# Where the weight sums of the seven-product stages are made: from SBUF during the second block to a table in HBM during the first

## The reference

```
for l in range(2):                       # first block
    h = rmsnorm(x); proj = h @ w_in[l]   # q k v g, sb sc sx, ca cb, three gates of 1024
    y_ret, y_sc, y_cf = retention(q,k,v), short conv, long conv + layernorm
    merged = sum of sigmoid(gate_b) * (y_b @ w_b)
    x = x + rmsnorm(merged @ w_o[l])
    up = causal_dwconv(rmsnorm(x) @ w_up[l])
    x = x + rmsnorm((silu(gate) * val) @ w_down[l])
for l in range(2):                       # second block
    h = rmsnorm(x); proj = h @ w_in_2[l] # u v z_a, c_q c_kv k_rope z_b, x_c z_c, g_a g_b g_c
    y_a = gmlp_spatial(u, v) * silu(z_a)
    y_b = mla_attention(c_q, c_kv, k_rope) * silu(z_b)
    y_c = rg_lru(x_c) * silu(z_c)
    merged = sum of sigmoid(g_b) * (y_b @ w_proj_b)
    x = x + rmsnorm(merged @ w_out[l])
```

## Time and profile before

| | us |
|---|---|
| median of 3 runs | 3138.83 |
| lowest and highest | 3138.8, 3139.8 |
| the profiled execution, its own time | 3137.91 |
| its span in the trace | 3136.6 |
| PE busy | 3120.1 |
| PEld, DVE, ACT, POOL busy | 2636.8, 1981.9, 1328.2, 574.4 |

### The profile page before, as it was taken

One profiled execution on the slowest core, in us unless ns is written; L12 is line 12 of the kernel. 1 busy time (PEld: TensorE's weight loads), 2 busy tenths in 40 slices (PEclk: granted clock), 3 DMA queues, 4 the chain that ended last, 5 costly groups with the idle time before them and its releaser, 6 DMA issues.

```text
span 3136.6 us, 38506 instructions
## 1 busy us (share of the span) xinstructions
PE 3120.1 (99%) x15368; PEld 2636.8 (84%) x15368; DVE 1981.9 (63%) x2664; ACT 1328.2 (42%) x2075; POOL 574.4 (18%) x427
## 2 busy tenths in 40 slices
PE   9999999999999999999999999999999999999999
PEld 8888888888888888888888888888888878888887
DVE  6876456665687655656558765457856766455774
ACT  4333334344333334433445542236745544233762
POOL 1201212110020111111013330130221332131031
PEclk9999999999999999999999999999999999999999
DMA  4322223235442233232552263223442254223423
GB/s 169 118 97 98 96 100 108 94 111 204 150 121 94 94 101 113 89 101 94 201 172 89 92 179 101 85 98 114 124 172 96 86 150 133 95 87 101 139 96 135
DMA packets 109938, 368.39 MB, mean 117 GB/s; under 512 B 14336, under 2 KB 14592, under 8 KB 108480
## 3 DMA queue, kind: packets, MB, share of 16 engines
q1 hardware_dynamic: 101280, 326.37, 31.5%
q0 software_dynamic: 8336, 39.03, 4.2%
q10 hardware_dynamic: 144, 0.52, 0.1%
HBM read 343.32 MB, written 6.29 MB: 111 GB/s over the span
## 4 chain that ended last, share of the span: by engine, by line
PE 95%; DVE 2%; DMA 1%; ACT 1%; issue 1%; POOL 0%; SPq 0%; ACTq 0%; POOLq 0%
PE ps L651 94%; DMA f<-wst 1%; PE ps L742 1%; PE ps L1067 0%; DVE r L1821 0%; DVE wl L1811 0%; ACT wh L1194 0%; DVE f L1826 0%; DMA X<-x_in 0%; DVE f L1889 0%; ACT f L1607 0%; SPq L2784 0%; DVE sm L2329 0%; POOL f L2718 0%; DVE r L2303 0%
## 5 line engine op out<-in xcount | busy, mean ns | idle before, releaser
L651 PE MATMUL ps<-h,wh 128*128 128x512 f32 (+1 forms) x5696 | 1609.5, 368 | 0.7
L651 PEld LDWEIGHTS ps<-h,wh 128*128 128x128 f32 x5696 | 1029.9, 188 | 182.2 <-issue 3.4
L651 PE MATMUL ps<-h,wl 128*128 128x512 f32 (+1 forms) x2848 | 1046.1, 367 | 0.0
L1811 DVE TENSOR_TENSOR wl<-raw,wh 128x1024 fp32r<-128x1024 f32 (+2 forms) x547 | 683.0, 1259 | 229.8 <-ACT wh L1194 229.2
L1194 ACT CAST wh<-raw 128x1024 fp32r<-128x1024 f32 (+2 forms) x560 | 553.1, 1003 | 428.4 <-PE ps L651 425.4
L651 PEld LDWEIGHTS ps<-h,wl 128*128 128x128 f32 x2848 | 534.6, 188 | 89.1
L651 PE MATMUL ps<-r,wh 128*128 128x512 f32 x1536 | 474.4, 390 | 1.0 <-DVE r L1821 0.5
L1291 ACT CAST r<-f 128x512 fp32r<-128x512 f32 x194 | 119.1, 620 | 513.8 <-DVE f L2222 149.0
L651 PEld LDWEIGHTS ps<-r,wh 128*128 128x128 f32 x1536 | 284.9, 188 | 59.0 <-issue 2.2
L651 PE MATMUL ps<-r,wl 128*128 128x512 f32 x792 | 304.3, 389 | 0.0
L651 PE MATMUL ps<-wh,r 128*128 128x512 f32 x960 | 302.7, 390 | 0.1
(11 more groups left out here) (205 smaller groups left out, 2905.0 us busy)
## 6 DMA issues: line engine op xcount, KB each, us to landing
raw<-wst SPq DMA_DIRECT2D x540, 512.0 KB, 3.4
f<-wst POOLq DMA_DIRECT2D x32, 512.0 KB, 7.4
raw<-wst SPq DMA_DIRECT2D x48, 320.0 KB, 2.9
r<-r SPq DMA_DIRECT2D x64, 128.0 KB, 2.3
f<-gains POOLq DMA_DIRECT2D x6, 1024.0 KB, 5.2
raw<-wst SPq DMA_DIRECT2D x20, 256.0 KB, 2.9
f<-f SPq DMA_DIRECT2D x72, 64.0 KB, 2.0
f<-tab POOLq DMA_DIRECT2D x16, 256.0 KB, 4.5
```

The costliest lines, as they stand in the source:

```text
L651: return e.matmul(o, a, b, start=start, stop=stop, skip_group_check=True)
L1811: e.tensor_tensor(l[:, 0:WIDTH[c]], sources(c)[0], h[:, 0:WIDTH[c]].bitcast(F32), ALU.subtract).then_inc(*lo_cut.up(("lo", c)))
```

## The change

The sums are made in HBM, and all chunks come through raw:

- The host packs two tables: wst with the plain chunks, and wpr with 24 blocks (8 gate pairs and 4 for v in each layer) of 128 x 2048, four pieces of 512 columns.
- A table wsum of the same shape lies in HBM. In the first block POOL runs `sum_slot` behind the first six additions of each gated branch and behind each of the 22 products of a feed-forward part, until 50 slots are done. An even slot copies block p from wpr to wsum and adds one piece of block p - 1; an odd slot adds two or three pieces. Each slot waits until the one before has landed.
- SP's `load` takes chunks from wst, wpr or wsum; from wsum after "summed". A pair is now four chunks (1024, 1024, 512, 1024 columns), v is 14 chunks of 1024.
- ACT and DVE cut every chunk whole and from raw. A raw slot is free after its lo cut. `sums`, `va_load`, `va_add`, `released`, `sources` and the f tiles go; `add_gated` in the second block runs unbroken, and the table loads ln stand ahead of ws.

```diff
+TERM = {"p1": (0, 0), "p2": (0, 1), "n5": (1, 1), "u2": (1, 0), "p3": (2, 0), "u3": (3, 1), "c21": (3, 0)}
+VA_ROWS = [("p1", "wpr", 512), ("p2", "wpr", 1024), ("n5", "wsum", 512), ("u2", "wsum", 0), ("p3", "wpr", 0), ("u3", "wsum", 1536),
+           ("c21", "wsum", 1024)]
...
+        wsum = nc.dram_tensor("wsum", (len(BLOCKS), P, 2 * CH), F32, kind="Internal").ap()
...
-                    if c in VA_SUM:
-                        w.wait_ge(*at("va_summed", CHUNKS[c][0]))
-                    elif PART.get(c) != 3:
-                        r = RAW_OF[c] + PART.get(c, 0) // 2
-                        w.wait_ge(s_raw[r % NRAW], 16 * (r // NRAW + 1))
+                    w.wait_ge(s_raw[c % NRAW], 16 * (c // NRAW + 1))
...
-                    if c not in PART:
-                        e.copy(h[:, 0:WIDTH[c]], sources(c)[0]).then_inc(*hi_cut.up(("hi", c)))
-                        continue
-                    for i, f in enumerate(sources(c)):
-                        if i or PART[c] == 3:
-                            w.wait_ge(*at("sums", CHUNKS[c][0][:-2], PART[c]))
-                        e.copy(h[:, i * S:(i + 1) * S], f).then_inc(*hi_cut.up(("hi", c, i)))
+                    e.copy(h[:, 0:WIDTH[c]], source(c)).then_inc(*hi_cut.up(("hi", c)))
...
-            def sums(name):
...
+            def sum_slot():
+
+                n, (p, second) = slots[0], divmod(slots[0], 2)
+                if p > len(BLOCKS):
+                    return
+                slots[0] += 1
+                if n:
+                    w.wait_ge(*at("sums", n - 1))
+
+                def add(p, to, source, event):
+                    e.dma_start(wsum[p, :, to:to + S], source, accum_op=ALU.add).then_inc(*added.up(("sums", n), event))
+
+                if second and p < len(BLOCKS):
+                    add(p, 512, wpr[p, :, 1536:2048], ("one", p))
+                    add(p, 1536, wpr[p, :, 0:512], ("three", p))
+                if second and p:
+                    add(p - 1, 1024, wsum[p - 1, :, 0:512], ("summed", p - 1))
+                if not second and p < len(BLOCKS):
+                    e.dma_start(wsum[p], wpr[p]).then_inc(*added.up(("sums", n)))
+                if not second and p:
+                    add(p - 1, 0, wsum[p - 1, :, 512:1024], ("two", p - 1))
...
+                    if L < 2 and j < 6:
+                        sum_slot()
...
                     e.tensor_tensor(F(t + 1), F(t), F(t + 1), ALU.mult).then_inc(*pool_tile.up(("f_prod", L, j)))
+                    sum_slot()
...
-                for c in range(2):
-                    va_add(1, c, f"va1_{c}", ("va_begun", L, 1, c), ("va_summed", f"{L}/vs1_{c}"))
...
+            def load(c):
+
+                name, pieces = CHUNKS[c]
+                dst, n = raw[:, c % NRAW, 0:WIDTH[c]], len(pieces)
+                if len(pieces[0]) != 4:
+                    src = wst[ROW_OF[name], :, 0:WIDTH[c]]
+                else:
+                    place, p, col, m = pieces[0]
+                    if place == "wsum":
+                        for i in range(n):
+                            w.wait_ge(*at("summed", p + i))
+                    src = (wsum if place == "wsum" else wpr)[p:p + n, :, col:col + m].rearrange("b p c -> p b c")
+                    dst = dst.rearrange("p (b c) -> p b c", b=n)
+                e.dma_start(dst, src).then_inc(s_raw[c % NRAW], 16)
...
-                    for event in released(c - NRAW):
-                        w.wait_ge(*at(*event))
+                    w.wait_ge(*at("lo", c - NRAW))
```

More of the change, by code:

```diff
@@ L171, in plan @@
         output(L, "w_out_2", l)
-    return out
+    return out, blocks
 def width(chunk):
-    return sum(P if p[4] == "lru" else p[4][1] - p[4][0] for p in chunk[1])
+    return sum(p[3] if len(p) == 4 else P if p[4] == "lru" else p[4][1] - p[4][0] for p in chunk[1])
 def vec_map(items):
@@ L191 @@
 NV = max(NV1, NV2)
[L193 to L221, removed]
-NRAW, NSP, LA = 4, 4, 2
-def released(r):
-    c = RAW_OF.index(r) if r in RAW_OF else RAW_OF.index(r - 1)
-    if c not in PART:
[L229 to L242, removed]
+CHUNKS, BLOCKS = plan()
+NAME = {name: c for c, (name, _) in enumerate(CHUNKS)}
+WIDTH = [width(chunk) for chunk in CHUNKS]
+PLAIN = [chunk for chunk in CHUNKS if len(chunk[1][0]) != 4]
+ROW_OF = {name: r for r, (name, _) in enumerate(PLAIN)}
+PAIRS = [name for name, _ in BLOCKS if "gate" in name]
+NRAW, NSP, LA = 4, 4, 2
 SLOT, FURTHER = CH + 64, 16
@@ L835, in gate_proj, with product @@
                     last.then_inc(*group_done.up(("done", key), *closes))
[L837 to L841, removed]
+            def product(key, name, what, xs, start=False, stop=False):
+                q, second = TERM[what]
+                h, l = weights(f"{name}*{q}")
+                o = bank(key)
                 for k, (xh, xl) in enumerate(xs):
@@ L844, in product @@
                     last = three(o[:, halves(0)], h[:, col:col + P], l[:, col:col + P], xh, xl, start and k == 0, stop and k == 3)
-                return last
+                ends = (("closed", NAME[f"{name}*{CLOSES[what]}"]),) if what in CLOSES else ()
+                last.then_inc(*group_done.up(("done", (name, what)), *ends))
             def two_tiles(L, name, between):
-                c = NAME[f"{name}*0"]
-                first, second, third = (take((name, i)) for i in "abc")
-                product(first, name, 0, 0, quarter(0, 0), True).then_inc(*group_done.up(("done", (name, "p1"))))
+                first, second, third = ((name, i) for i in "abc")
@@ L852, in two_tiles @@
+                for key in (first, second, third):
+                    take(key)
+                product(first, name, "p1", quarter(0, 0), True)
                 for m in "1643":
                     w.wait_ge(*at("mixed_lo", L, m))
-                product(second, name, 0, 1, combined("1"), True).then_inc(*group_done.up(("done", (name, "n5")), ("closed", c)))
-                product(third, name, 1, 0, quarter(0, 1), True, True).then_inc(*group_done.up(("done", (name, "p2"))))
+                product(second, name, "n5", combined("1"), True)
@@ L867, in two_tiles, with va_product @@
                 between(2)
-            def va_product(L, acc, rows, chunks, what, xs, start=False, stop=False, after=None):
-                names = [f"{L}/{rows}{c}" for c in chunks]
+            def va_product(L, acc, what, xs, start=False, stop=False, after=None):
+                names = [f"{L}/va_{what}{c}" for c in range(2)]
                 keys = [("va", L, acc, t) for t in range(2)]
@@ L2820, in sync @@
                     spread(*SPREAD_AT[c])
-                e.dma_start(raw[:, c % NRAW, 0:width(RAWS[c])], wst[c, :, 0:width(RAWS[c])]).then_inc(s_raw[c % NRAW], 16)
+                load(c)
                 if c == 1:
```

181 lines of the change are left out of this document (68 added, 113 removed).

## The result

The changed kernel takes 3172.65 us (median of 4 runs, 3170.94 to 3173.1), the kernel before beside it 3138.82: a ratio of 1.0107, interval 1.0089 to 1.0124. The forecast was 3128, with a range up to 3151. The time is 34 us longer and outside the range; the first rival is what happened.

The account below looks back on a forecast made before the run. TensorE (PE) was taken to bound the kernel, busy 3120.1 of 3136.6 us, so only its waits could change. From 3137.91 us, -11.1 (second block) + 0.4 (slots) gave 3127.2; median 3128, range 3125 to 3151.

Parts of the forecast that it names:

- the first rival: First block: slots land late, GpSimd holds its adds back and PE waits at both mixers' ends; slower, chance 0.33.
- v stage, -9.9 us: Second block, two layers: v products no longer wait for sums made in SBUF; 43.4 + 43.5 - 2 x 38.5 = 9.9 us gained.
- Gate pairs, -1.2 us: Second block: GpSimd's 64 additions go, and with them VectorE's slow lo cuts; 2 x 0.59 = 1.2 us gained.
- More loads, a smaller ring, at nothing: Second block: more chunks per gate pair and v stage through the four-deep raw ring, costed at nothing.
- The slots, +0.4 us: First block, 46 of 50 slots in two mixers and one feed-forward part: they fit narrowly, loss 0, with 0.4 us allowed.
- 3e + 2o below 45.1 us, 9.0 each: Mixer's last branch: five landings, three even (e) and two odd (o), must fit 45.1 us; expected 43.9, 1.2 to spare.
- e = 8.7 and o = 8.9: Start to landing in us: even slot 2.1 + 3.1/0.72 + 2.25 (fixed, 1 MB copy, 256 KB accumulation), odd 2.1 + 6.75.
- 402.4: First mixer's last branch: latest start in us of the sixth add's slot that keeps the eighth add in time at 406.7.
- The forecast's chain from POOL's add over ScalarE's cast to PE: First mixer's end: eighth add 406.74, cast 408.44, weight chunk's lo cut 410.05 to 411.27, PE 411.38; PE has no slack.
- The feed-forward part, 11.2 us each: First block's feed-forward part: 21 landings must fit into 217.5 + 18.4 us, or 11.2 us each.
- Each us above costs 2: First rival's rate: each us by which five landings exceed 45.1 costs 2 us over both mixers; break-even at 50.7.
- the forecast's fixed part: Any transfer's landing: 2.1 us independent of size, read from 1 MB landing in 5.2 and 2 MB in 8.3.

Follow-up runs that it names:

- the combination: Changed kernel with accumulating transfers of 32 rows of 8 KB, and slots moved to mixers' first branches and nineteen per feed-forward part: 3124.99 us.

## Why the prediction was wrong

**v stage, -9.9 us: right.** 43.4 + 43.5 became 2 x 38.20, which is 10.5.

**Gate pairs, -1.2 us: right.** 6.24 became 5.65. ScalarE has 48 instructions fewer and VectorE 48, and not 64 and 68; they are off the path either way. Together with the v stage 11.1 was forecast, and the kernel without slots is 11.3 faster.

**More loads, a smaller ring, at nothing: right.** No wait of PE on a load, a cast or a cut appears in the second block of the kernel without slots.

**The slots, +0.4 us: wrong, 47.6.** The step that failed is "3e + 2o below 45.1 us, 9.0 each", and in it the assumption that issuing costs only the instruction's own time. In place of e = 8.7 and o = 8.9 the slots take 9.4 and 12.8 us in the mean, because every third accumulating transfer stands at its issue. The limit was right, and so, less closely, were e and o as prices of a transfer: slots without a wait at issue take 8.27 and 10.00 (o is 1.1 dearer than forecast), so 3e + 2o = 44.8; with 0.3 us from each landing to the next start, for which the forecast had no term, it would be 46.3, 1.2 over. What the five slots of the first mixer's last branch took is 357.24 to 414.67, 57.4 us: two of them hold a wait at issue, and they take 15.7 and 12.7 us to the landing where free ones take 10.0 and 8.3. That is 12.3 past 402.4. The sixth slot's own last issue is held as well, and the seventh add starts at 421.36, 4.0 later than 414.67 + 2.7 of issuing. Together 16.3 us, and PE waited 15.75. The forecast's chain from POOL's add over ScalarE's cast to PE was right link by link.

The kernel before did show a wait at issue. POOL's timeline in its v stage:

```profile
1799.36 1.84 POOL L2718 DMA_DIRECT2D f<-wst  x2
1800.50 1.83 POOL L2730 DMA_DIRECT2D f<-gmb  x2
1807.90 0.90 POOL L2718 DMA_DIRECT2D f<-wst  x1 [5.57 <-issue]
1811.23 0.88 POOL L2718 DMA_DIRECT2D f<-wst  x1 [2.43 <-issue]
...
1826.37 0.88 POOL L2718 DMA_DIRECT2D f<-wst  x1 [4.58 <-issue]
```

I read only the landings of these transfers as their cost. The row to read was the idle time in front of the issue. It would have warned of the wait, but not given its size: there each wait ends when the oldest transfer in flight has landed. The two of 1799.36 land at 1807.64 and 1810.97, 0.26 us before the two held ones start, with three others still in flight both times.

**The feed-forward part, 11.2 us each: the limit was the wrong kind.** The 21 landings took 497.07 to 738.63, 11.5 each, so 5.7 us over 235.9; but PE waited 12.1 us, since it was first held at 649.69, long before the sum over the whole part ran out. Two slots of 14 us stood behind each other there (633.80 and 647.89, to 661.91), against 21.8 us for two products. A limit on the mean holds only as long as the lead it starts with; after that, each pair of slots must fit beside its own products.

**Clock.** I gave the clock no term in the first block. It is 9.5 us, a fifth of the loss.

**The rivals.** "Each us above costs 2" is what happened: 15.75 and 10.17 us in the two mixers. Its price was for dearer copies, and the copy is not the culprit (e without a wait was below the forecast). It came through another door, one that doubles nothing and only puts transfers behind each other. So the rival was right on who waits and at what rate, and wrong on why the slots are late.

The Trainium skill's rate for copies between two HBM tensors (DMA: Bandwidth & Descriptors, Latency and other measured facts) was measured on the sync and scalar queues, and not on GpSimd's; it gave by estimate 3140 us, nearer to the result than mine. The trace doesn't bear it out here: the 1 MB copy lands in a median 6.1 us, 5.4 to 8.5, where the page's rate gives by estimate 4.9 and with the forecast's fixed part 7.0; the forecast's own 2.1 + 4.3 is nearer. The estimate was nearer by luck, since nothing of the 47.6 us is shown to come from the copy.

**Open.** How much the room holds and what frees it is not settled. Counted from one wait at issue to the next, three accumulating transfers and a copy (464 packets by the count above) pass in the changed kernel, and in the kernel with 256 rows two of them (544 packets) never do. But in the v stage of the kernel before, five transfers of 592 packets in all are in flight before GpSimd is first held. There it waits for the oldest in flight; in the changed kernel it waits for all, even where that is one copy. Why the two differ is not known, and a larger room beside four raw buffers wasn't tried. What is shown is that the waits and their cost go down with more room, and their number with fewer rows.

## What to carry to other kernels

A queue has room as well as speed: before more transfers are put on GpSimd's queue, count the rows that they add to it (here by all transfers since the last wait, and not by those in flight), and look in the trace for idle time "<-issue" between transfers issued on end. Where it stands, make the rows longer (contiguous tables) or the room larger, before moving anything. And place work that holds an engine's queue behind instructions that nobody waits for soon: here the last branch before a projection was the worst place, and the first branch cost nothing that a run shows. The time beside which such work must fit is read from the rows of the stage where it runs: two products gave 21.8 us and not the 22.8 that was assumed, and a pair of slots takes 22.

## What the runs showed of the hardware

- A GpSimd transfer can be held at issue without any semaphore: with 1 KB per partition set aside, about every third accumulating transfer of 128 rows waits, and it starts 0.26 to 0.42 us after the last in flight has landed. In the kernel before it starts 0.26 us after the oldest has. With 4 KB the waits fall from 21 to 7, with 32 rows per transfer from 21 to 6, with 256 rows they rise to 69.
- The price of HBM-to-HBM accumulation is moderate: 2.55 us per 256 KB in a slot of three with rows of 1 and 2 KB, near the 2.25 read from accumulations into on-chip memory. With 32 rows of 8 KB such a slot takes 7.85 us in place of 10.00.
- A plain load behind such transfers pays as well: the 1 MB loads of gains land in 10.0 us, against 5.2 before, and in 5.4 in the combination, where the slots end earlier.
